# Attention scores of two heads as products over 64 rows each, on separate halves of TensorE

## The reference, cut to what matters

```
s = einsum('bqhd,bqkhd->bhqk', q, k) * D ** -0.5 + bias      # D = 64, bias = -slope * distance
s = where(valid, s, -inf);  lse = logsumexp(s);  p = exp(s - lse)
o = einsum('bhqk,bqkhd->bqhd', p, v)
```

## Time and profile before

| | |
|---|---|
| median of 3 runs | 1908.58 us |
| the profiled execution | 1912.45 us, of which the span is 1910.6 us |
| TensorE matmul busy | 1854.7 us, 97% |
| TensorE weight load busy | 1813.8 us, 95% |
| VectorE, ScalarE, GpSimd busy | 754.5, 601.8, 528.5 us |
| mean granted TensorE clock | 0.985 |
| attention passes | 603 to 943 us of the span |

### The profile page before, as it was taken

One profiled execution on the slowest core, in us unless ns is written; L12 is line 12 of the kernel. 1 busy time (PEld: TensorE's weight loads), 2 busy tenths in 40 slices (PEclk: granted clock), 3 DMA queues, 4 the chain that ended last, 5 costly groups with the idle time before them and its releaser, 6 DMA issues.

```text
span 1910.6 us, 28747 instructions
## 1 busy us (share of the span) xinstructions
PE 1854.7 (97%) x11954; PEld 1813.8 (95%) x11954; DVE 754.5 (39%) x1466; ACT 601.8 (31%) x1301; POOL 528.5 (28%) x308
## 2 busy tenths in 40 slices
PE   6899999999999999999989999999999999999998
PEld 6899999999999999999989999999999999999997
DVE  5752741832822232333275226511451154115413
ACT  5523423523524243334334333311230132113211
POOL 1222121131131011111135445422442244224342
PEclk9899999999999999989999999999999999999999
DMA  5232222222234244545533332211221122112212
GB/s 159 80 83 58 91 71 89 73 75 88 65 104 155 66 131 147 153 139 172 179 124 120 90 101 67 83 50 45 66 78 53 47 78 67 45 49 84 67 45 91
DMA packets 235835, 173.13 MB, mean 91 GB/s; under 512 B 16277, under 2 KB 225250, under 8 KB 235322
## 3 DMA queue, kind: packets, MB, share of 16 engines
q1 hardware_dynamic: 200586, 131.51, 23.4%
q10 hardware_dynamic: 35120, 39.80, 6.3%
HBM read 133.97 MB, written 47.72 MB: 95 GB/s over the span
## 4 chain that ended last, share of the span: by engine, by line
PE 86%; DVE 8%; ACT 2%; DMA 1%; issue 1%; POOL 0%; SPq 0%; DVEq 0%; ACTq 0%; POOLq 0%
PE dense L207 42%; PE dense L232 26%; PE work L1409 2%; PE work L1429 1%; DVE conv L803 1%; PE work L1046 1%; PE work L1457 1%; PE work L1053 1%; DVE summed L1789 1%; PE work L1440 1%; PE work L1401 1%; ACT gates L1655 1%; PE work L995 1%; PE work L411 1%; DVE summed L1786 1%
## 5 line engine op out<-in xcount | busy, mean ns | idle before, releaser
L196 POOL TENSOR_TENSOR WL<-Wraw,WH 128x1024 fp32r<-128x1024 f32 (+1 forms) x131 | 316.0, 2412 | 1044.1 <-ACT WH L191 969.4
L232 PE MATMUL dense<-hH,WH 128*128 128x352 f32 x1128 | 393.3, 349 | 2.8 <-POOL WL L196 2.8
L232 PE MATMUL dense<-hH,WL 128*128 128x352 f32 x1128 | 369.6, 328 | 0.0
L232 PE MATMUL dense<-hL,WH 128*128 128x352 f32 x1128 | 369.0, 327 | 0.0
L207 PE MATMUL dense<-hH,WH 128*128 128x352 f32 x1008 | 326.4, 324 | 2.7 <-POOL WL L196 2.7
L207 PE MATMUL dense<-hL,WH 128*128 128x352 f32 x1008 | 323.1, 321 | 0.0
L207 PE MATMUL dense<-hH,WL 128*128 128x352 f32 x1008 | 323.0, 320 | 0.0
L191 ACT ACTIVATE WH<-Wraw 128x1024 fp32r<-128x1024 f32 (+1 forms) x131 | 136.2, 1040 | 361.5 <-PE dense L207 296.3
L207 PE MATMUL dense<-gH,WH 128*128 128x352 f32 x768 | 247.5, 322 | 1.6 <-DVE gL L1805 0.8
L207 PE MATMUL dense<-gL,WH 128*128 128x352 f32 x768 | 247.8, 323 | 0.0
L207 PE MATMUL dense<-gH,WL 128*128 128x352 f32 x768 | 247.8, 323 | 0.0
(11 more groups left out here) (311 smaller groups left out, 2481.6 us busy)
## 6 DMA issues: line engine op xcount, KB each, us to landing
Wraw<-in_w_in SPq DMA_DIRECT2D x51, 512.0 KB, 4.1
Wraw<-in_w_up SPq DMA_DIRECT2D x32, 512.0 KB, 4.1
Wraw<-in_w_down SPq DMA_DIRECT2D x32, 512.0 KB, 3.8
cache<-in_cache_win SPq DMA_DIRECT2D x20, 512.0 KB, 6.6
qkv_scratch<-fill ACTq DMA_DIRECT2D x54, 176.0 KB, 1.9
raw<-qkv_scratch SPq DMA_DIRECT2D x6, 1584.0 KB, 7.9
out_win_s<-in_cache_win ACTq DMA_DIRECT2D x16, 512.0 KB, 3.7
gb_scratch<-fill ACTq DMA_DIRECT2D x24, 176.0 KB, 2.6
```

The lines of the kernel that those rows point to most:

```text
L196: G.tensor_tensor(WL[:, s, 0:k], Wraw[:, s, 0:k], WH[:, s, 0:k].bitcast(F32), ALU.subtract).then_inc(sem("w_split"), 1)
L232: ins = PE.matmul(dense[t][:, 0:TN], w[:, s, k, :], x[:, k, TN * t:TN * t + TN], start=(k == 0 and i == 0), stop=(k == KD - 1 and i == 2))
```

## The change

The scores of head e are computed from partitions 64e to 64e+63 of q and k alone, into the bank `work[e]`; block n uses columns 0 to 255 or 256 to 511 by its parity. The prompt part of `aq[:, 1]` is not made any more, and `aq[:, 0]` is q scaled without a mask there; the masked rows stay for the 32 sample tokens. VectorE reads the scores from the new places. The number of increments of `aq_set` in a pass stays two.

```diff
 # att_scalar
             if g:
                 src, n = by_residue(raw[:, 0], g)
-                A.activation(grouped(aq[:, 0], n), src, ACT.Copy, scale=q_scale[:, 0:1])
-                for e in range(2):
-                    ins = A.activation(aq[:, e, TP:T], raw[:, 0, TP:T], ACT.Copy, scale=q_scale[:, e:e + 1])
-                ins.then_inc(sem("aq_set"), 1)
+                A.activation(grouped(aq[:, 0], n), src, ACT.Copy, scale=-HB ** -0.5).then_inc(sem("aq_set"), 1)
             else:
-                for e in range(2):
-                    A.activation(aq[:, e], raw[:, 0], ACT.Copy, scale=q_scale[:, e:e + 1]).then_inc(sem("aq_set"), 1)
+                A.activation(aq[:, 0, 0:TP], raw[:, 0, 0:TP], ACT.Copy, scale=-HB ** -0.5).then_inc(sem("aq_set"), 1)
+            for e in range(2):
+                ins = A.activation(aq[:, e, TP:T], raw[:, 0, TP:T], ACT.Copy, scale=q_scale[:, e:e + 1])
+            ins.then_inc(sem("aq_set"), 1)
 # att_vector
                 if g:
-                    if s:
-                        src, n = by_residue(raw[:, 0], g)
-                        V.tensor_scalar(grouped(aq[:, 1], n), src, q_scale[:, 1:2], None, ALU.mult).then_inc(sem("aq_set"), 1)
                     src, n = by_residue(raw[:, 1 + s], g)
...
                     for e in range(2):
-                        V.tensor_tensor_reduce(prob[:, n % 2, e, 0:w], work[n % 2][:, 2 * P * e:2 * P * e + w], bias_p[:, e, 2 * P - w:2 * P],
+                        V.tensor_tensor_reduce(prob[:, n % 2, e, 0:w], work[e][:, 2 * P * (n % 2):2 * P * (n % 2) + w], bias_p[:, e, 2 * P - w:2 * P],
 # att_tensor
                     for e in range(2):
-                        k = keys_of(aq[:, 2], g, n) if is_wide(g, n) else block_of(aq[:, 2], g, n)
-                        ins = PE.matmul(work[n % 2][:, 2 * P * e:2 * P * e + w], block_of(aq[:, e], g, n), k, start=True, stop=True)
+                        r, c = slice(HB * e, HB * e + HB), 2 * P * (n % 2)
+                        k = keys_of(aq[r, 2], g, n) if is_wide(g, n) else block_of(aq[r, 2], g, n)
+                        ins = PE.matmul(work[e][:, c:c + w], block_of(aq[r, 0], g, n), k, start=True, stop=True)
                     ins.then_inc(sem("scores"), 1)
```

## The result

Over 20 runs each, the changed kernel took 1912.81 us (1907.98 to 1916.09) and the kernel before 1908.12 us (1904.15 to 1913.49): ratio 1.0023, 95% interval 1.0015 to 1.0031, so 2.9 to 5.9 us slower. The direction was as predicted, the size about a third of it (+4.4 against +11.9 us); 1912.81 us lies at the lower edge of 1912 to 1930 and outside the 1915 to 1926 of the forecast itself.

A forecast was written before the change was run, and what follows sets the result against it. TensorE, busy for 97% of the span, was taken as the bound. Half-array trips, overlap and preparation summed to 18.2 - 4.8 - 1.5 = +11.9 us, taking the median from 1908.58 to 1920.5 us; range 1912 to 1930, the forecast's own 1915 to 1926.

The forecast's parts named there:

- Part 1: Score products on TensorE: going into and out of the half array costs 0.38 us in each of 48 blocks, +18.2 us.
- The floor of 0.23: Lower bound in us per block for going into and out of the half array, from transposes of prob_s on 64 rows.
- no change: Outcome too near the kernel before to tell: a measurement can tell about 0.2%, 3.8 us; chance of same 0.04.
- Part 2: Two heads' score products side by side on TensorE: 0.216 us saved per wide block, nothing in narrow ones, -4.8 us.
- The sign named for a wide block: In wide blocks' scores, head 0's second matmul and head 1's first start within some 10 ns.
- the upper bound, 7.7 us: Most that score overlap could save: 0.216 us in 22 wide blocks, 0.112 us in 26 narrow ones.
- Part 3: Preparation of q: dropping VectorE's masked copy saves 1.1 us at group 1's start, shorter prob waits 0.4; -1.5 us taken.
- Part 4: Score banks: both heads' banks written in every block add no wait, 0 us.
- A: Rival for the score products: the halves do not overlap, +16.7 us, 1925.3 us; chance 0.17.
- B: Rival for the scores: nothing runs empty, matmuls and loads of the halves overlap, -9.2 us, 1899.4 us; chance 0.10.
- C: Rival in the attention stage: new slices under full clock between 603 and 943 us; chance 0.09, size not in the text.
- D: Rival for the scores: cheap way in and out, 0.23 us for both, every overlap, +1.8 us, 1910.4 us; chance 0.04.

The follow-up runs named there:

- same_half: Changed kernel with both heads' score products taken from partitions 0 to 63, head 1's scores replaced by head 0's: 1925.39 us, ratio 1.0092 to the kernel before.
- by_half: Changed kernel with two blocks' scores per trip into the half array, both products of half 0 first, then both of half 1: 1899.61 us, ratio 0.9957.
- pairs: Changed kernel with the scores of two blocks issued in one trip into the half array, 24 trips for 48, heads alternating: 1898.6 us, ratio 0.9952.
- pairs_full: Kernel before, full-array products with masked copies, but two blocks' scores issued together and banks laid out by head: 1908.0 us, ratio 0.9995.
- split: Changed kernel with the transposes of k and v between a block's two score products, 96 trips into the half array for 48: 1941.7 us, ratio 1.0179.

## Why the prediction was wrong in size

Its direction rested on Part 1, and Part 1 was right. The way in and out of the half array was put at 0.38 us a block from runs on 32 rows; the block loops of two unlike groups give 0.39, the removal of visits 0.38. The floor of 0.23 taken from the 64-row transposes was not needed. The signs came where the prediction said: "issue" idle before the first score load, and before the dense load behind it in wide blocks, with 0.12 us there in narrow ones. Still, that the direction came out owes something to luck. With the overlap as it was measured, the same sum is +1.4 us, within what the prediction called no change. And 1912.81 us lies inside the stated range because the range was wide, not because its sum of +11.9 was near.

The step that failed is Part 2, the size of the overlap: 4.8 us predicted, 14.8 measured by same_half (15.3 if one whole product of two is hidden in every block). Two assumptions in it were wrong. The first was that matmuls start in program order over both halves, so that only one of a block's four could be hidden; by_half and pairs differ by 0.2 us in their loops, so the order had no influence that can be told, and the starts show both passes of both heads paired (607.852 with 607.858, 608.065 with 608.072). The sign named for a wide block was the second matmul of head 0 beside the first of head 1; what came was first beside first and second beside second. The second was that loads of 128 columns go one by one at 0.112 us, taken from full-array products in one stream; loads of different halves overlap as well (four in 0.30 us where four full-array ones took 0.53). What I called the upper bound, 7.7 us, was therefore no bound: it allowed one hidden matmul in a block, and two of the four are hidden. With 15.3 in place of 4.8 the prediction's sum reads 18.2 - 15.3 - 1.5 = +1.4 us.

How close the halves run is in the starts: 6 to 7 ns between the two matmuls of a pair in the changed kernel, 12 to 14 in by_half. A load also ran beside the matmuls of its own half: in same_half products on one half still keep the pace of their matmuls (0.71 us for four, with 0.10 of it the bare first load). Inside a visit, behind its first load, two matmuls took the time of one: in by_half a pair of 256 columns takes 0.218 us (608.122 to 608.340), where one full-array matmul takes 0.216. That the array runs empty at each change was the prediction's reading; what the traces show is 0.09 us more from the last matmul of one kind to the first of the other. In the changed kernel it is 0.20 us from the second transpose to the first score matmul (607.649 to 607.852) and from the last score matmul to the first dense one (608.072 to 608.273), where the pace is 0.11 for transposes and for narrow score matmuls. The first load that nothing hides, 0.10 us each way (0.213 us from the first score matmul to its head's second, 0.265 from the first dense matmul to the second, where 0.11 and 0.16 are the pace), makes up the rest of the 0.39 us.

Part 3 was right: 1.0 us for the one wait, 1.1 predicted; about 0.5 us for the waits for exp, 0.4 predicted. Part 4 was right: pairs_full measures banks and order at nothing.

Of the rivals, A (no overlap) is out: same_half is that kernel and takes 1925.39 us, where A said 1925.3. B had the overlap more nearly right (7.7 us for 14.8 measured) and the way in and out wrong (under 0.10 us each for the 0.19 to 0.20 that V gives); against it stood the 0.10 us lost before a transpose whose load has 64 rows and 128 columns (656.18 to 656.44, where dense matmuls follow each other at 0.16). C, stretches at the lower clock in the block loops, did not happen in the two traces of the changed kernel, whose block loops run at 1.00 throughout; one came in one execution of split. The slowest execution of the changed kernel took 1916.09 us, so no run comes near the 1930 up to which the range takes C in. D had small terms on both sides and came nearest in time with two wrong sizes.

Loops (+3.0) and start of group 1 (-1.0) give +2.0 us. The measured difference is 2.9 to 5.9 us in the first series and 1.3 to 4.8 in the second. The rest, 1 to 2.4 us at the middle of the two, must lie outside the block loops, where stretches at the lower clock come and go. The mean granted clock recorded for each execution allows an estimate: the lower level is half of the full one (0.50 granted, and dense matmuls 0.29 us apart there for 0.16) and TensorE is the bound, so one minus this clock, times the span, is about what the clock cost. That gives 29.0 us over the 31 executions of the changed kernel, 28.0 over the 47 of the kernel before that ran beside the experiments, and 25.6 over the six of `pairs`. Without this part the changed kernel is 2.7 us longer than the kernel before (1.6 to 3.8), which agrees with +2.0; the clock's part of +1.0 (-0.3 to +2.3) cannot be told from nothing. Against `pairs` it can: 3.4 us (2.1 to 4.8), beside 9.9 us without it, where the loops have 9.2. Why the clock takes more from the changed kernel than from `pairs` stays open.

## What to carry to other kernels

Two products on 64 rows each, on different halves of the array, cost the time of one here, loads included, in both orders tried: a pair of matmuls took 0.11 us with 128 columns and 0.22 with 256, as one full-array matmul does. But going into the half array and out of it cost TensorE 0.39 us for the round trip, so put several such products into one visit: here a visit had to hide more than 0.39 us of product time, one narrow block hides 0.22, one wide 0.43, two blocks 0.45 to 0.86. Before taking a change of shape as free or as lost, count the round trips separately from the products.

## What the runs showed of the hardware that was not expected

- Within a visit, the order in which matmuls and loads of the two halves were written made no difference: eight matmuls in 0.93 us with the heads alternating and with the heads one after the other.
- A weight load on one half still overlapped the matmuls of the same half: in same_half three of the four matmuls follow each other at 0.11 us, with loads of 0.19 us beside them.
- The share of time at the lower clock level differed between executions of one kernel: a stretch of 118 matmuls between block loops took 23 us in one (mean granted clock 0.78) and 20 us in another (0.91). One execution of split stayed at a granted clock of 0.50 for 24 us in a loop that kept TensorE busy (24.00 of 24.00 us), and took 1953.57 us where its four fellows took 1940.39 to 1943.5.
